# Gated layers of a one-core transformer kernel: two pairs of chunks as seven block products

## The reference

```python
def swiglu(h, wg, wu, wd):
    return (jax.nn.silu(h @ wg) * (h @ wu)) @ wd
...
    for l in range(DEPTH_2):
        g = norm_g[l]
        h = rmsnorm(x, g[0])
        x = x + 0.5 * rmsnorm(swiglu(h, ffn_wg[l, 0], ffn_wu[l, 0], ffn_wd[l, 0]), g[1])
        ...
        h = rmsnorm(x, g[4])
        x = x + 0.5 * rmsnorm(swiglu(h, ffn_wg[l, 1], ffn_wu[l, 1], ffn_wd[l, 1]), g[5])
```

## Time and profile before

| | |
|---|---|
| runs | 1432.56 us median of 3 (1432.13 to 1433.68) |
| profiled execution | span 1431.2 us, 1.4 us under the median |
| PE | busy 1392.6 us, 97% of the span |
| DVE, ACT | 926.0 us and 758.1 us, 65% and 53% |
| first and third gated layer, from the transposes of chunk 1 to the last chunk | 154.2 and 154.3 us |
| clock of PE in them | 1.00 of full speed |

### The profile page before, as it was taken

How to read it: one execution, slowest core, us unless ns; L and a number is a source line. 1 busy time by engine, 2 the same in 40 slices (tenths; PEclk the granted TensorE clock), 3 DMA queues, 4 the chain that set the end, 5 groups by cost and what they waited for, 6 DMA issues and landing times.

```text
span 1431.2 us, 19205 instructions
## 1 busy us (share of the span) xinstructions
PE 1392.6 (97%) x7039; PEld 1157.8 (81%) x7039; DVE 926.0 (65%) x1401; ACT 758.1 (53%) x1249; POOL 79.3 (6%) x133
## 2 busy tenths in 40 slices
PE   4999999999999999999899999999999999999998
PEld 4878877999988888887778888888888877788886
DVE  5677787799777554479986555476545556675453
ACT  4456746755456444366576444465444467574442
POOL 3011100000000000021300000000000100000000
PEclk9999999999999999999999999999999999999999
DMA  9887656477645765544355765547555373565550
GB/s 352 279 293 263 195 173 195 146 268 245 227 146 176 231 196 181 177 133 148 118 173 178 226 199 181 176 134 257 183 185 197 121 210 118 191 230 182 188 165 30
DMA packets 177596, 274.36 MB, mean 192 GB/s; under 512 B 6465, under 2 KB 120897, under 8 KB 177505
## 3 DMA queue, kind: packets, MB, share of 16 engines
q1 hardware_dynamic: 170800, 250.87, 53.2%
q0 software_dynamic: 5552, 20.20, 4.6%
q10 hardware_dynamic: 1153, 2.07, 0.4%
HBM read 272.05 MB, written 1.06 MB: 191 GB/s over the span
## 4 chain that ended last, share of the span: by engine, by line
PE 78%; DVE 4%; issue 1%; ACT 1%; POOL 0%; DVEq 0%; POOLq 0%; ACTq 0%
PE psum L2552 22%; PE psum L2554 22%; PE psum L2553 22%; PE psum L2595 2%; PE psum L2594 2%; PE psum L2592 2%; PE psum L2797 1%; DVE w_lo L2147 1%; PE psum L2649 1%; PE psum L2721 1%; PE psum L2750 0%; DVE attn L2324 0%; PE psum L2664 0%; DVE work L2301 0%; PE psum L2703 0%
## 5 line engine op out<-in xcount | busy, mean ns | idle before, releaser
L2147 DVE TENSOR_TENSOR w_lo<-raw,w_hi 128x1024 fp32r<-128x1024 f32 (+1 forms) x312 | 371.9, 1235 | 115.4 <-ACT w_hi L1936 114.5
L2552 PE MATMUL psum<-w_hi,hT_hi 128*128 128x512 f32 x888 | 357.3, 402 | 6.4 <-DVE hT_lo L2247 3.7
L1936 ACT ACTIVATE w_hi<-raw 128x1024 fp32r<-128x1024 f32 (+1 forms) x312 | 310.8, 1050 | 98.6 <-PE psum L2554 62.2
L2554 PE MATMUL psum<-w_hi,hT_lo 128*128 128x512 f32 x888 | 347.8, 392 | 0.0
L2553 PE MATMUL psum<-w_lo,hT_hi 128*128 128x512 f32 x888 | 347.3, 391 | 0.0
L2552 PEld LDWEIGHTS psum<-w_hi,hT_hi 128*128 128x128 f32 x888 | 167.8, 189 | 45.5 <-issue 10.2
L2554 PEld LDWEIGHTS psum<-w_hi,hT_lo 128*128 128x128 f32 x888 | 167.5, 189 | 36.5
L2553 PEld LDWEIGHTS psum<-w_lo,hT_hi 128*128 128x128 f32 x888 | 168.1, 189 | 32.8 <-issue 0.5
L2147 DVE TENSOR_TENSOR lo_qk<-raw,hi_qk 128x1024 fp32r<-128x1024 f32 (+1 forms) x72 | 84.1, 1209 | 32.5 <-ACT hi_qk L1936 31.8
L2552 PE MATMUL psum<-w_hi,hc_hi 128*128 128x512 f32 x256 | 100.3, 392 | 0.6 <-DVE hc_lo L2472 0.6
L2554 PE MATMUL psum<-w_hi,hc_lo 128*128 128x512 f32 x256 | 99.8, 390 | 0.0
(11 more groups left out here) (236 smaller groups left out, 2335.5 us busy)
## 6 DMA issues: line engine op xcount, KB each, us to landing
raw<-in_ffn_wg_dram SPq DMA_DIRECT2D x88, 512.0 KB, 4.0
raw<-in_ffn_wu_dram SPq DMA_DIRECT2D x88, 512.0 KB, 5.0
raw<-in_ffn_wd_dram SPq DMA_DIRECT2D x44, 1024.0 KB, 5.0
raw<-in_w_up_dram SPq DMA_DIRECT2D x44, 512.0 KB, 4.9
raw<-in_w_in_dram SPq DMA_DIRECT2D x19, 1024.0 KB, 7.5
ada_raw<-in_w_ada_dram POOLq DMA_DIRECT2D x24, 512.0 KB, 5.1
raw<-in_even_w_in_dram SPq DMA_DIRECT2D x12, 1024.0 KB, 5.1
raw<-in_odd_w_in_dram SPq DMA_DIRECT2D x12, 1024.0 KB, 5.5
```

The source lines that it names most:

```text
L1936: nc.scalar.activation(hi_of(s)[:, cs], raw_of(s)[:, cs], ACT.Copy).then_inc(ready, 1)
L2147: nc.vector.tensor_tensor(lo_of(u)[:, cs], raw_of(u)[:, cs], hi_of(u)[:, cs].bitcast(F32), ALU.subtract)\
L2552: nc.tensor.matmul(o, a_hi, b_hi, start=start, stop=False)
L2554: return nc.tensor.matmul(o, a_lo, b_hi, start=False, stop=stop)
```

## The change

In each of the four gated layers chunks 4 and 5 are made together, and 7 and 8 (`GROUPS`). Their gate and up sums are one product: 256 tokens by 1024 inputs, times 1024 inputs by 1024 columns (512 gate, 512 up). Cut in two each way that is 8 block products of 128 tokens, 512 inputs and 512 columns; the change makes it from 7 (Winograd's form). With X11, X12 the two input halves of the first 128 tokens, X21, X22 those of the second, g0, g1 the gate weights of the two input halves and u0, u1 the up weights, the seven weight blocks are, in PE's order:

| name here | weights | made by | tokens | bank (chunk 4) |
|---|---|---|---|---|
| U1 | g0 | loaded | X11 | 4 |
| U5 | u0+g0 | DVE sum, 2 halves | X22-X21 | 5 |
| U7 | u0+u1 | DVE sum | X11-X21 | 6 |
| U2 | g1 | loaded | X12 | 4, on top of U1's |
| U6 | u0+g0+u1 | DVE sum | X11+X22-X21 | 7 |
| (D3) | down unit of chunk 3 | | | |
| U3 | u1 | from the `raw` slot of U7 | X11+X22-X21-X12 | 5, on top of U5's |
| U4 | u0+g0+u1+g1 | DVE sum | X22 | 6, on top of U7's |

Each takes a unit's place in the ring of five and 12 matmuls. Behind U4 come A and B, the up units of chunk 6, then D4 and D5, the down units of the pair. The mixed tokens are made once a layer (`token_rows`, `token_sums`, `token_high`, `token_low`). `gkeep`, `gsum`, `gup` and `ggate` combine the banks; `gturn` turns the hidden rows of the pair, 128 tokens at a time. In the diff `self.down(c - 2)` of a group is D4.

```diff
+GROUPS = (4, 7)
...
-            for c in range(2, NFC - 1):
+            c = 2
+            while c < NFC - 1:
+                if c in GROUPS:
+                    self.group(c)
+                    c += 2
+                    continue
+                after_group = c - 2 in GROUPS
                 self.up(c, 0)
+                if after_group:
+                    self.group_turn(c - 2, 0)
                 self.up(c, 1)
+                if after_group:
+                    self.group_turn(c - 2, 1)
                 self.out(c)
+                if c == 2:
+                    pl.add("token_sums")
+                    pl.add("token_high")
+                if after_group:
+                    self.down(c - 2)
                 self.down(c - 1)
                 self.hidden_turn(c)
+                if c == 2:
+                    pl.add("token_low")
+                c += 1
+
+        def group(self, c):
...
+            banks = (4, 5, 6, 7) if c % 2 == 0 else (6, 7, 4, 5)
+            u1 = pl.unit(4, BANK, [(0, BANK, block(gate, 0))])
+            u5 = pl.sum_unit(block(up, 0), "sums", "own", u1)
+            u7 = pl.sum_unit(block(up, 4), u5, u5, "own")
+            u2 = pl.unit(4, BANK, [(0, BANK, block(gate, 4))])
+            u6 = pl.sum_unit(None, "sums", "sums", u7)
+            pl.release[u1], pl.release[u5] = u5, u7
+            p1, p5, p7 = (pl.use(b, u) for b, u in zip(banks, (u1, u5, u7)))
+            product_of(u1, p1, True, tile=(0, 0), mixed=None)
+            product_of(u5, p5, True, tile=None, mixed=3)
+            pl.add("gkeep", use=p1, slot=0)
+            product_of(u7, p7, True, tile=None, mixed=2)
+            pl.add("gkeep", use=p5, slot=1)
+            p2 = pl.use(banks[0], u2)
+            product_of(u2, p2, False, tile=(4, 0), mixed=None)
+            pl.add("ggate", t=0, use=p2, stat=self.st, n=n)
+            p6 = pl.use(banks[3], u6)
+            product_of(u6, p6, True, tile=None, mixed=0)
+            pl.add("gsum", kept=(p1, p5), uses=(p6, p7), n=n)
+            self.down(c - 1)
+            u3 = pl.unit(4, BANK, [])
+            pl.raw_from[u3], pl.release[u7] = u7, u3
+            p3 = pl.use(banks[1], u3)
+            product_of(u3, p3, False, tile=None, mixed=1)
+            pl.add("gup", use=p3, gate=p2, stat=self.st, n=n)
+            u4 = pl.sum_unit(None, "sums", "sums", u2)
+            pl.release[u2] = u4
+            p4 = pl.use(banks[2], u4)
+            product_of(u4, p4, False, tile=(4, 1), mixed=None)
+            pl.add("ggate", t=1, use=p4, stat=self.st, n=n)
...
-                        sp.wait_ge(hi_ready, number + 1)
-                        sp.wait_ge(lo_ready, number + 1)
+                        until = plan.release.get(number, number)
+                        sp.wait_ge(hi_ready, until + 1)
+                        sp.wait_ge(lo_ready, until + 1)
...
                 if s >= len(units):
                     return
+                form(s + 1)
                 for half in range(2):
                     split_lo_half(s, half)
...
+                a, b = (blended if v == "sums" else raw_of(v) for v in (made["a"], made["b"]))
+                for half in range(2):
+                    cs = half_of(u, half)
+                    nc.vector.tensor_tensor(source_of(u)[:, cs], a[:, cs], b[:, cs], ALU.add).then_inc(sum_ready, 1)
```

More of the change, by code:

```diff
@@ L152, in unit, with sum_unit @@
         return len(self.units) - 1
+    def sum_unit(self, load, dst, a, b):
+        u = self.unit(4, BANK, [(0, BANK, load)] if load is not None else [])
+        a, b = (u if isinstance(v, str) and v == "own" else v for v in (a, b))
+        last = self.last_sum if dst == "sums" else None
+        if isinstance(b, int):
+            self.formed[u] = dict(by="vector", no=self.n_formed, dst=dst, a=a, b=b, last=last)
+            self.n_formed += 1
+        else:
+            self.formed[u] = dict(by="dma", no=self.n_landed, dst=dst, src=b, last=last)
+            self.n_landed += 1
+        if dst == "sums":
+            self.last_sum = u
+        return u
     def use(self, bank, unit=None, read_by=None, by_unit=False):
@@ L245, in load_order @@
         for kind, a in self.steps:
-            if kind == "split_hi" and a["unit"] < len(self.units):
+            if kind == "split_hi" and a["unit"] < len(self.units) and self.units[a["unit"]][2]:
                 order.append(("w", a["unit"]))
@@ L879, in go_on, with block, product_of @@
                 self.out(c)
+                if c == 2:
[3 more added lines that the diff above has]
+                    self.down(c - 2)
                 self.down(c - 1)
                 self.hidden_turn(c)
+                if c == 2:
+                    pl.add("token_low")
+                c += 1
+        def group(self, c):
+            gate, up = self.gate_up
+            n = pl.n_group
+            pl.n_group += 1
+            def block(w, k0):
+                return rows(w, k0, 4, c * FC, BANK)
+            def product_of(u, use, start, **of):
+                pl.split_ahead(u)
+                pl.add("gprod", unit=u, use=use, start=start, **of)
+            banks = (4, 5, 6, 7) if c % 2 == 0 else (6, 7, 4, 5)
[28 more added lines that the diff above has]
+            pl.add("ggate", t=1, use=p4, stat=self.st, n=n)
+            self.group_no = n
@@ L883, in halves, with group_turn @@
+        def group_turn(self, c, t):
+            made = pl.turned_use((7 if c % 2 == 0 else 5) - t)
+            pl.add("gturn", c=c, t=t, n=self.group_no, down_before=self.downs[c - 1], **made)
+            self.gs[c, t] = self.gs[c + 1, t] = made["g"]
         def halves(self, t, half):
@@ L906, in tail @@
             c = NFC - 1
-            self.up(c, 0)
+            if c - 2 in GROUPS:
+                self.units[c] = self.up_units(c, (0,))
+                self.down_unit(c - 2)
+                self.units[c] += self.up_units(c, (4,))
+                self.open(c)
+                p = self.parts[c][0]
+                pl.split_ahead(p["unit"])
+                product_step("up", p, ks=(0, 1), inc=None)
+                for t in range(TT):
+                    self.group_turn(c - 2, t)
+                product_step("up", p, ks=(2, 3))
+                self.down_part(c - 2)
+            else:
+                self.up(c, 0)
             second = self.parts[c][1]
@@ L1555, in program @@
         PR = sb("PR", [P, TT * EVEN_W])
+        end = nc.sbuf_base
+        mixed_hi = over("mixed_hi", end, TT * EVEN_W - UNIT, UNIT)
+        mixed_lo = over("mixed_lo", end, TT * EVEN_W - 2 * UNIT, UNIT)
         gate_rows = sb("gate_rows", [P, 2, D])
@@ L1717, in raw_of, with source_of @@
             return raw[:, raw_slot["w", u], 0:width(u)]
+        def source_of(u):
+            if u in plan.formed:
+                dst = plan.formed[u]["dst"]
+                return blended if dst == "sums" else raw_of(dst)
+            return raw_of(plan.raw_from.get(u, u))
         def half_of(u, half):
@@ L1824, in _ @@
                     load_half(0, 1)
+                elif kind == "split_hi":
+                    made = plan.formed.get(a["unit"])
+                    if made is not None and made["by"] == "dma":
+                        pool.wait_ge(hi_ready, made["last"] + 1)
+                        pool.wait_ge(lo_ready, made["last"] + 1)
+                        pool.dma_start(blended.rearrange("p (k n) -> p k n", k=4), made["src"], accum_op=ALU.add)\
+                            .then_inc(sum_landed, 16)
                 elif kind == "ada" and a["own"] is not None:
@@ L2137, in split_lo, with form @@
                     return
+                form(s + 1)
                 for half in range(2):
                     split_lo_half(s, half)
+            formed = set()
+            def form(u):
+                if u not in plan.formed or u in formed or plan.formed[u]["by"] == "dma":
+                    return
+                formed.add(u)
+                made = plan.formed[u]
+                for v in (made["a"], made["b"]):
+                    if v != "sums" and (v not in plan.formed or v == u or ("w", v) in raw_slot):
+                        dve.wait_ge(weight_loaded[raw_slot["w", v]], landed["w", v])
+                if made["last"] is not None:
+                    dve.wait_ge(hi_ready, made["last"] + 1)
+                    dve.wait_ge(lo_ready, made["last"] + 1)
+                if made["no"]:
+                    dve.wait_ge(sum_ready, 2 * made["no"])
+                a, b = (blended if v == "sums" else raw_of(v) for v in (made["a"], made["b"]))
+                for half in range(2):
+                    cs = half_of(u, half)
+                    nc.vector.tensor_tensor(source_of(u)[:, cs], a[:, cs], b[:, cs], ALU.add).then_inc(sum_ready, 1)
             def split_lo_half(u, half):
@@ L2537, in _ @@
             split_seen, units_seen = [0], [(-1, 1)]
+            n_mixed = [0]
             def need_group(g):
```

165 lines of the change are left out of this document (153 added, 12 removed).

## The result

The changed kernel takes **1463.28 us** (median of four runs, 1460.91 to 1467.58), the kernel before 1433.12 beside it: ratio 1.0214, 95% interval 1.0197 to 1.0232. It is 2.1% slower; 1459.0 was forecast, 1437 to 1475 the range.

The account below looks back on a forecast made before the run. PE was taken to bound the kernel, with DVE and ACT waiting for it. Waits of 12.1 us less 5.45 saved give 6.65 a layer, +26.6 over four layers: 1459 us, range 1437 to 1475.

Parts of the forecast that it names:

- What bounds the kernel: In the gated layers PE works without waits at full clock, 16.80 us a chunk; DVE and ACT wait for it.
- What it removes: Up products of each pair: 84 matmuls for 96, saving 2.73 us a pair, 5.45 a layer, 21.8 in all.
- What it adds: For each pair on DVE: three more splits and four sums at 2.28 us each, plus gsum, gup and ggate.
- The schedule of the first pair: Chunks 4 and 5: DVE idles 4.35 us on A's load; gup frees the bank at 63.3, PE wants it at 58.1.
- t = 0: Zero of the predicted schedule: where PE starts the up products of chunk 2.
- The waits: PE waits in both pairs: 5.15 up to A, 2.95 at D4, 2.6 and 0.25 in the second pair; 11.0 a layer.
- The clock: Behind the waits ahead of A (3.75) and in the second pair (2.6), 1.3 us lost each; 1.1 a layer more in total.
- Rival 3: In the gated layers the clock falls after every wait, short ones too, and loads queue: 1481 us, chance 12%.
- The sum: Waits of 12.1 less 5.45 saved is 6.65 us a layer, four layers alike: +26.6 us.
- A's late data: At A's raw slot: the load starts after U3's split, data there at 52.6, leaving DVE idle 4.35 us ahead of gup.
- rival 1: At A's raw slot: with data there in time DVE keeps ahead, gup done at 57.7; gain 14, time 1418, chance 10%.

Follow-up runs that it names:

- experiment 7: Changed kernel with gup ahead of B's and D4's halves, U3's halves ahead of U4's sum, gturn ahead of the next pair's halves: 1422.98 us, ratio 0.9936.
- experiment 8: Changed kernel with pairs at chunks 7 and 8 only, gup ahead of the halves and U3's halves ahead of U4's sum: 1426.92 us, ratio 0.9961.
- experiment 1: Changed kernel with gup moved ahead of B's and D4's halves on DVE: 1462.03 us, ratio 1.0204.
- experiment 12: Changed kernel with gturn ahead of the next pair's halves and U3's halves ahead of U4's sum, gup not moved: 1462.93 us, ratio 1.0203.
- experiment 4: Changed kernel with eight unused matmuls behind U4's product to keep PE at work in the wait ahead of A: 1461.21 us, ratio 1.0200.
- experiment 11: Changed kernel with gup ahead of B's and D4's halves, plus 14 unused matmuls ahead of chunk 4's second turn: 1464.41 us, ratio 1.0217.
- experiment 2: Changed kernel with U3 using U6's weights so A's raw slot is released earlier, and U3's halves ahead of U4's sum: 1450.92 us, ratio 1.0127.
- experiment 5: Changed kernel with U3's halves made ahead of U4's sum, so A's transfer starts 2.3 us earlier: 1449.78 us, ratio 1.0119.

## Why the prediction was right, and where it was not

*What bounds the kernel.* Right: PE had no waits in these stretches, and the change gave it some.

*What it removes.* 96 matmuls and 21.8 us. Experiments 7 and 8 bear it out within 3 us. With 9.3 us of listed waits and one stretch of 1.7 us, experiment 7 should come to -21.8 + 9.3 + 1.7 = -10.8. Its four layers, cut as above, take 131.82, 131.48, 131.27 and 134.92 us, -8.1 against before; the span is 10.1 shorter, but 2.1 of that lie ahead of the first gated layer, where nothing was changed. Experiment 8, with half the pairs and 3.1 us of waits, should come to -7.8 and comes to -6.6 in the layers.

*What it adds.* DVE's sums take what the split takes: `scr<-raw` x2 2.36 against 2.35 for `lo_at` x2, in experiment 1's rows. DVE's work in the window of a layer grows from 73.3 to 115.8 us.

*The schedule of the first pair.* The transfer was sized well: DVE idle ahead of A 4.35 predicted, 4.42 measured, and 4.28 to 4.46 in seven of the eight pairs. The eighth, the second pair of layer 1, has 5.43, and behind it is the wait of 3.47 ahead of chunk 9 where the other layers have 2.6 to 2.7. With t = 0 at 460.97, U3's halves end at 46.6 (47.2 predicted) and `gup` frees the bank at 62.7 (63.3). By its fit for a DMA from GpSimd the Trainium skill ("DMA: Bandwidth & Descriptors", "Anatomy of one DMA") gives an estimate of 4.4 us for 1 MB; this transfer is issued by SP as two DMAs of 512 KB, and takes 5.04 from the issue of the second to ACT's start.

*The waits.* All four are at the places named. Means over the layers against the prediction: ahead of U4 1.29 (1.4); ahead of A 3.09 (3.75); at D4 1.23 (1.6, after what the clock takes out of it); ahead of chunk 9 2.85 (2.6). Their sum, 8.5 a layer, is 0.9 below the 9.35 forecast. The prediction took the four layers as alike; their sums go from 7.56 to 9.61.

*The clock.* This is the mis-sized term. The prediction charged 1.3 us behind each of two waits, 2.6 gross a layer. The runs show a loss of 1.7 us behind some waits, up to 2.9 behind one, and none behind others of the same length: 13.0 us while PE was running in four layers, 3.2 a layer. Both the price and the rule could have been read better in the trace of before. Its windows begin at 702, but the clock had fallen before that, while PE waited:

```profile
701.00:702.00 1.00, 0.29 (x2) 0.33 (x3) 1.00 (x4) 0.00 (x0) 0.28 (x1) 0.62 0.00 0
704.00:705.00 1.00, 1.00 (x5) 0.86 (x4) 0.93 (x3) 0.67 (x2) 0.00 (x0) 0.68 0.00 0
```

With 702 to 704 at 0.50 that is a stretch of 3.4 us, as in the layers after, with 1.5 us lost from PE's start at 701.71. And the wait at 701.71 is not the only one of this size inside the kernel, as the prediction has it. Another of 2.94 us, in its first part, was followed by full clock:

```profile
88.62 1.10 PE L2632 MATMUL psum<-ada_acc,ones 128*128 128x512 f32 x2 [2.94 <-issue]
```

```profile
88.62:92.62 4.00, 4.00 (x16) 2.97 (x17) 4.00 (x11) 0.00 (x0) 0.71 (x1) 1.00 0.88 292
```

So the trace of before already had one such wait with a fall and one without. Rival 3, a fall after every wait, did not come in the changed kernel (its layer 4 has four waits and one fall), but it nearly did in experiment 12. The Trainium skill ("TensorE: Matmul & The Clock Gate", "HAM oscillation") has the clock fall at such gaps every time round; in the rows above two gaps of 3.47 us disagree about that, and experiments 4 and 11 agree in so far as shorter waits left fewer falls.

*A term left out.* A printed wait counts from the modelled end of the matmul ahead (0.39 us after its start, where the pitch is 0.23), so each of them costs 0.16 more: from 519.89 to 523.75 is 3.86, less 0.23 is 3.63, against 3.47 in the bracket.

*The sum.* For four layers: waits 33.8, four times four handovers of 0.16 2.6, clock 13.0, less 21.8 = 27.6, against 30.9 measured. The 3 us left were not added up from rows; stalls under 0.3 us are the likely place. The forecast was +26.6. So it came within 4.3 us with waits a little too long (0.9 a layer) and the clock, the handovers and the small stalls too short; part of the nearness is luck, in that these cancel.

*The reason.* The prediction took A's late data, at the head of the queue ahead of `gup`, for the cause that would decide the sign: with it early, a gain of 14 us (rival 1). That gain was summed wrongly. Its 57.7 for `gup` also takes away the 1.3 us ahead of U2, and its 1.6 at D4 is a wait shortened by a loss of the clock that this rival does not have. By the schedule itself, A's data alone brings `gup` to 63.3 - 4.35 = 58.95, 0.85 after PE wants it; with 2.95 at D4 and 0.25 the waits are 4.05 a layer, the gain 5.6, the time 1427. Experiments 1, 2 and 5 show that the cause, too, was too simple. With A's idle time nearly gone (0.24, experiment 2) the time is still 1450.9. In DVE's order B and D4 stand ahead of `gup`, and the next pair's sum stands ahead of `hc_lo`; B and that sum have transfers of their own to wait for (2.27 and 2.12 us). Only the three together give the gain that rival 1 had at one place: 1423, where it had 1418. Not tried: another raw slot, and an order in which D4's second turn is early too.
